# A top-2-of-8 expert layer: tokens as the stationary operand, weights streamed 512 columns wide as rounded high and low halves

## The reference

```
probs = softmax(h @ w_router);  top_p, top_i = top_k(probs, 2);  top_p /= sum(top_p)
gates = sum(one_hot(top_i, 8) * top_p)
out = sum over the 8 experts e of gates[e] * ((silu(h @ wg[e]) * (h @ wu[e])) @ wd[e])
```

## Time and profile before

| | us |
|---|---|
| median of three runs (2529.94 to 2535.5) | 2533.66 |
| the profiled execution: its time | 2536.45 |
| its span in the trace | 2534.8 |
| TensorE busy (87% of the span) | 2208.2 |
| VectorE busy (28%) | 713.9 |
| ScalarE busy (20%) | 515.2 |
| first expert matmul starts at | 1815.36 |
| last store of expert rows is issued at | 2486.20 |
| mean granted TensorE clock over the span | 0.901 |

### The profile page before, as it was taken

One profiled execution on the slowest core, in us unless ns is written; L12 is line 12 of the kernel. 1 busy time (PEld: TensorE's weight loads), 2 busy tenths in 40 slices (PEclk: granted clock), 3 DMA queues, 4 the chain that ended last, 5 costly groups with the idle time before them and its releaser, 6 DMA issues.

```text
span 2534.8 us, 35841 instructions
## 1 busy us (share of the span) xinstructions
PE 2208.2 (87%) x14774; PEld 1990.0 (79%) x14774; DVE 713.9 (28%) x1347; ACT 515.2 (20%) x1094; POOL 242.6 (10%) x325
## 2 busy tenths in 40 slices
PE   5899898976769999997898699997699999999992
PEld 4788787864659999996654576686699999999991
DVE  2245555537232222222234344402100000000003
ACT  1133422203022212211123233301211111111101
POOL 0000101020002302300020023200100000000001
PEclk8899999956789999998898689977799999999996
DMA  7222100030213242332070256510788988898883
GB/s 192 69 67 75 35 1 4 1 95 26 83 33 92 72 113 76 88 103 71 15 245 1 67 193 237 179 50 1 202 216 211 267 211 211 208 271 215 209 203 123
DMA packets 452952, 306.17 MB, mean 121 GB/s; under 512 B 22381, under 2 KB 435456, under 8 KB 448704
## 3 DMA queue, kind: packets, MB, share of 16 engines
q1 hardware_dynamic: 433812, 225.76, 34.2%
q0 software_dynamic: 19024, 78.72, 9.4%
HBM read 276.44 MB, written 28.14 MB: 120 GB/s over the span
## 4 chain that ended last, share of the span: by engine, by line
PE 66%; issue 19%; DVE 6%; POOL 4%; DMA 2%; SPq 1%; ACT 1%; POOLq 0%; DVEq 0%; ACTq 0%
PE bank L1197 17%; PE bank L526 13%; PE bank L1226 8%; PE bank L1038 3%; POOL actL L2220 2%; PE bank L706 2%; PE bank L691 1%; PE bank L701 1%; PE bank L1052 1%; PE bank L1079 1%; PE bank L564 1%; POOL actH L2217 1%; SPq L2311 1%; PE bank L857 1%; PE bank L859 1%
## 5 line engine op out<-in xcount | busy, mean ns | idle before, releaser
L1197 PE MATMUL bank<-arena,w_ring 128*128 128x176 f32 x2816 | 424.4, 314 | 4.8 <-issue 4.8
L1197 PEld LDWEIGHTS bank<-arena,w_ring 128*128 128x128 f32 x2816 | 422.3, 191 | 6.8 <-issue 6.8
L526 PE MATMUL bank<-hT,w_ring 128*128 128x260 f32 x1600 | 362.8, 389 | 16.2 <-DVE hT L1249 15.1
L526 PEld LDWEIGHTS bank<-hT,w_ring 128*128 128x128 f32 x1600 | 309.3, 194 | 66.0 <-DVE hT L1249 16.0
L1790 ACT ACTIVATE arena<-bank 128x512 f32<-128x512 f32 (+5 forms) x284 | 135.7, 494 | 511.5 <-PE bank L526 225.6
L1226 PE MATMUL bank<-arena 128*128 128x176 f32 x1408 | 220.1, 313 | 0.0
L1226 PEld LDWEIGHTS bank<-arena 128*128 128x128 f32 x1408 | 210.2, 190 | 0.2
L857 PE MATMUL bank<-hH,gu_high 128*128 128x260 f32 x704 | 143.6, 286 | 18.3 <-DVE w_low L1508 18.3
L1752 DVE TENSOR_TENSOR arena<-arena,bank 128x176 f32<-128x176 f32 x88 | 29.8, 338 | 431.6 <-PE bank L1197 431.6
L859 PE MATMUL bank<-hL,gu_high 128*128 128x260 f32 x704 | 143.0, 285 | 0.0
L861 PE MATMUL bank<-hH,w_low 128*128 128x260 f32 x704 | 142.9, 285 | 0.0
(11 more groups left out here) (440 smaller groups left out, 2884.6 us busy)
## 6 DMA issues: line engine op xcount, KB each, us to landing
w_ring<-in_we_gate SPq DMA_DIRECT2D x88, 512.0 KB, 7.2
w_ring<-in_we_up SPq DMA_DIRECT2D x88, 512.0 KB, 7.3
arena<-in_we_down SPq DMA_DIRECT2D x64, 704.0 KB, 6.6
w_ring<-in_w_in_a SPq DMA_DIRECT2D x26, 512.0 KB, 3.8
w_ring<-in_w_gate SPq DMA_DIRECT2D x22, 512.0 KB, 3.9
w_ring<-in_w_up SPq DMA_DIRECT2D x22, 512.0 KB, 3.9
arena<-in_w_down SPq DMA_DIRECT2D x16, 704.0 KB, 6.2
slots<-arena POOLq DMA_DIRECT2D x4, 2560.0 KB
```

The lines of the kernel that those rows point to most:

```text
L526: mm = pe.matmul(out[i][:, 0:hi - lo], w_ring[:, s, kt, :], rhs[:, kt, lo:hi], start=(kt == 0), stop=(kt == KT - 1))
L1197: mm = pe.matmul(bank[bk][:, 0:SLOTS], w_ring[:, s, kt, :], hTe[:, kt, :], start=(kt == 0), stop=(kt == KT - 1))
```

## The change

SLOTS becomes 192, so a pass is 128 tokens and a tail (TAIL) of 64. The roles in the matmul are exchanged: the tokens are the stationary operand, and the weights stream past, 512 columns (in the last piece 384) at a time.

- The weights of a pass come in 35 chunks instead of 30 blocks: 24 for gate and up (three pieces of the 1408 columns, 512, 512 and 384; a chunk has two row blocks of 128 for one piece) and 11 for down (128 rows of all 1024 columns). A row of a chunk is 512, 384 or 1024 floats in one run of memory; before, a run was 128 floats. The ring has RAWS = 18 slots of 1024 floats: the 11 of `w_ring`, and seven more in `hT` and `xT`, which are free by then.
- ScalarE rounds every chunk into one of HIGHS = 6 buffers (`high_part`), VectorE writes the remainder over the raw chunk (`low_part`). Both run EAHEAD = 4 chunks ahead of TensorE in the program's order; the four chunks that open the next pass are done at the end of the present one, those of the first pass ahead of the loop.
- The tokens, and later the activations, are transposed into tiles of twice SLOTS columns: 192 high, then 64 low of the tail, then 128 low of the first 128 tokens.
- A product of one 128-row block with one 512-column stretch is five matmuls (`products`): high tokens x high weights, low tokens x high weights, the tail's high and low together (128 stationary columns) x high weights, high tokens x low weights, the tail's high x low weights. The low half of the tail comes out on partitions 64 to 127 of its bank and is added later.
- At the end of each of the three pieces (chunks 7, 15 and 23), ScalarE and VectorE form silu(gate) x up for the 128 tokens and for the tail. TensorE transposes the result three or four chunks later (TURN_AFTER: after chunks 11, 19 and 26), and the next pass's tokens after chunks 28 and 30.
- Results come out as rows of tokens: the transposes of the results, and the copies around them, are gone. A pass's rows are written in two DMAs.
- SyncE no longer waits for the scatters ahead of the first weights, only for the table and for the last use of the slots by the output projection; the four first chunks go out ahead of the loop, the next fourteen as soon as the transposes of the stream are over.

```
-SLOTS = 176
+SLOTS = 192
 ROWS = SLOTS // 2
+TAIL = SLOTS - P
+PIECES = [(0, 512), (512, 1024), (1024, FE)]
+GU_CHUNKS = 8 * len(PIECES)
+CHUNKS = GU_CHUNKS + FB
+TURN_AFTER = {11: (0, 2), 19: (2, 4), 26: (4, 6), 28: (6, 8), 30: (8, 10)}
...
+ACT0 = DENSE_PARTS * 2 * FB + 1
+LAPS = CHUNKS + 1
+RAWS = LAPS // 2
+HIGHS = 6
+EAHEAD = 4
...
+        def raw_slot(m):
+            s = m % RAWS
+            if s < WS:
+                return w_ring[:, s].rearrange("p k c -> p (k c)")
+            rest, i = (hT, s - WS) if s < WS + 4 else (xT, s - WS - 4)
+            return rest.rearrange("p k t -> p (k t)")[:, i * D:(i + 1) * D]
...
-                        for kt in range(KT):
-                            mm = pe.matmul(bank[bk][:, 0:SLOTS], w_ring[:, s, kt, :], hTe[:, kt, :],
-                                           start=(kt == 0), stop=(kt == KT - 1))
...
+                    def products(out, tail, x, at, top, low, first, last):
+                        w = x[:, at]
+                        pe.matmul(out, w[:, 0:P], top, start=first, stop=False)
+                        pe.matmul(out, w[:, SLOTS + TAIL:WIDE], top, start=False, stop=False)
+                        pe.matmul(tail, w[:, P:SLOTS + TAIL], top, start=first, stop=False, skip_group_check=True)
+                        pe.matmul(out, w[:, 0:P], low, start=False, stop=last)
+                        return pe.matmul(tail[0:TAIL], w[:, P:SLOTS], low, start=False, stop=last, skip_group_check=True)
...
+                    for i, (lo, hi) in enumerate(PIECES):
+                        n = hi - lo
+                        at = 4 * (i % 2)
+                        if i == 1:
+                            pe.wait_ge(y_read, p * 4 + 4)
+                        if i == 2:
+                            pe.wait_ge(h_split, p * TURNS + KT + 4 + 2)
+                        for q in range(4):
+                            for k in range(2):
+                                kt = 2 * q + k
+                                c = slice(k * n, (k + 1) * n)
+                                for j in range(2):
+                                    m = 8 * i + 2 * q + j
+                                    if k == 0:
+                                        pe.wait_ge(split, p * LAPS + SPLIT0 + m + 1)
+                                    mm = products(bank[at + j][:, 0:n], bank[at + 2 + j][:, 0:n], hTw, kt, e_high[:, m % HIGHS, c],
+                                                  low_slot(m)[:, c], kt == 0, kt == KT - 1)
+                                    if k == 1:
+                                        mm.then_inc(e_used, 1)
+                            turns(m)
+                    pe.wait_ge(h_split, p * TURNS + KT + 4 + 4)
+                    for f in range(FB):
+                        m = GU_CHUNKS + f
+                        pe.wait_ge(split, p * LAPS + SPLIT0 + m + 1)
+                        pe.wait_ge(h_split, p * TURNS + KT + 4 + f // 2 + 1)
+                        for j in range(2):
+                            c = slice(512 * j, 512 * (j + 1))
+                            mm = products(bank[4 + j], bank[6 + j], actTw, f, e_high[:, m % HIGHS, c], low_slot(m)[:, c],
+                                          f == 0, f == FB - 1)
+                        mm.then_inc(e_used, 1 if f < FB - 1 else 2)
+                        turns(m)
...
+            def low_part(m, lap):
+                n = chunk_columns(m)
+                dve.wait_ge(high, lap + SPLIT0 + m + 1)
+                dve.tensor_tensor(low_slot(m)[:, 0:n], raw_slot(m)[:, 0:n], e_high[:, m % HIGHS, 0:n].bitcast(F32), ALU.subtract)\
+                   .then_inc(split, 1 if m < CHUNKS - 1 else 2)
...
+                dve.tensor_tensor(to[:, :, SLOTS:SLOTS + TAIL], v[:, :, P:SLOTS], to[:, :, P:SLOTS].bitcast(F32), ALU.subtract)
+                dve.tensor_tensor(to[:, :, SLOTS + TAIL:WIDE], v[:, :, 0:P], to[:, :, 0:P].bitcast(F32), ALU.subtract).then_inc(h_split, 1)
...
+                            dve.wait_ge(silu_done, p * 7 + 2 * i + 1)
+                            dve.tensor_tensor(actu[0:TAIL, 0:n], actu[0:TAIL, 0:n], tu[0:TAIL], ALU.add)
+                            dve.tensor_tensor(actg[0:TAIL, 0:n], actg[0:TAIL, 0:n], tg[0:TAIL], ALU.add).then_inc(act_split, 1)
+                            dve.tensor_tensor(acte[:, 0:n], acte[:, 0:n], bu, ALU.mult)
+                            dve.wait_ge(silu_done, p * 7 + 2 * i + 2)
+                            dve.tensor_tensor(actg[0:TAIL, 0:n], actg[0:TAIL, 0:n], actu[0:TAIL, 0:n], ALU.mult).then_inc(act_split, 1)
...
+                act.wait_ge(e_used, lap + RAWS + m - HIGHS + 1)
+                act.activation(e_high[:, m % HIGHS, 0:n], raw_slot(m)[:, 0:n], ACT.Copy)\
+                   .then_inc(high, 1 if m < CHUNKS - 1 else 2)
...
+                    for m in range(LAPS):
+                        if m + EAHEAD < CHUNKS:
+                            high_part(m + EAHEAD, p * LAPS, p)
+                        elif m + EAHEAD >= LAPS:
+                            high_part(m + EAHEAD - LAPS, p * LAPS + LAPS, p + 1)
...
+                            act.wait_ge(e_used, p * LAPS + RAWS + m + 1)
+                            act.activation(actg[0:TAIL, 0:n], tg[TAIL:P], ACT.Copy)
+                            act.activation(actu[0:TAIL, 0:n], tu[TAIL:P], ACT.Copy)
+                            act.activation(acte[:, 0:n], bg, ACT.Silu).then_inc(silu_done, 1)
+                            act.wait_ge(act_split, p * 6 + ACT0 + 2 * i + 1)
+                            act.activation(actg[0:TAIL, 0:n], actg[0:TAIL, 0:n], ACT.Silu).then_inc(silu_done, 1)
...
-            sp.wait_ge(spread, 160)
+            def expert_chunk(m, e):
+                dst = raw_slot(m)[:, 0:chunk_columns(m)]
+                if m < GU_CHUNKS:
+                    lo, hi = PIECES[m // 8]
+                    q = m % 8 // 2
+                    w = a["we_up" if m % 2 else "we_gate"][0][bass.ds(e, 1), 2 * q * P:2 * (q + 1) * P, lo:hi]
+                    load(dst.rearrange("p (k c) -> p k c", k=2), w.rearrange("a (k p) c -> p (a k) c", p=P), e_loaded[m % RAWS])
+                else:
+                    f = m - GU_CHUNKS
+                    w = a["we_down"][0][bass.ds(e, 1), f * P:(f + 1) * P, :]
+                    load(dst, w.rearrange("a p c -> p (a c)"), e_loaded[m % RAWS])
...
+            filled(sp, (("o", 1, KT - 1), 1))
+            for m in range(EAHEAD):
+                expert_chunk(m, e0)
...
+                    for m in range(EAHEAD, CHUNKS):
+                        if m != GU_CHUNKS:
+                            sp.wait_ge(e_used, p * LAPS + (m + 1 if m != GU_CHUNKS - 1 else m + 2))
+                        expert_chunk(m, e)
+                    after = sp.value_load(table[0:1, bass.ds(p + 1, 1)], min_val=0, max_val=NE - 1)
+                    for m in range(EAHEAD):
+                        sp.wait_ge(e_used, p * LAPS + LAPS + m + 1)
+                        expert_chunk(m, after)
```

More of the change, by code:

```diff
@@ L1168, in _, with turn_tokens @@
                     mm.then_inc(full("upto"), 1)
-            def expert_tokens(g, b):
+            for b in range(8):
+                pe.wait_ge(bank_free[b], uses[b])
+            pe.wait_ge(table_ready, 1)
+            n_passes = pe.value_load(table[0:1, PASSES + 1:PASSES + 2], min_val=1, max_val=PASSES)
+            def turn_tokens(g, at):
+                pe.wait_ge(h_split, at + KT - 1)
+                b = bank[TURN_BANK[6 + g]]
                 for j in range(2):
@@ L1174, in expert_tokens, with turn_act @@
                                           hrow[0:ROWS, r, (2 * g + j) * P:(2 * g + j + 1) * P], ident[0:ROWS, 0:ROWS])
-                mm.then_inc(hx, 1)
+                mm.then_inc(turned_out, 1)
+            def turn_act(g, at):
+                pe.wait_ge(h_split, at + KT - 1)
+                b = bank[TURN_BANK[g]]
+                lo = PIECES[g // 2][0]
+                for j in range(min(2, FB - 2 * g)):
+                    c = slice((2 * g + j) * P - lo, (2 * g + j + 1) * P - lo)
+                    pe.transpose(b[:, j * SLOTS:j * SLOTS + P], acte[:, c], ident)
+                    mm = pe.transpose(b[:, j * SLOTS + P:(j + 1) * SLOTS], actg[0:TAIL, c], ident[0:TAIL, 0:TAIL])
+                mm.then_inc(turned_out, 1)
@@ L1177, in _ @@
             pe.wait_ge(hrow_in, 16)
             for g in range(4):
[L1179 to L1187, removed]
+                turn_tokens(g, g)
@@ L1231, in _, with turns @@
-                    results(KT - 1)
+                    def turns(m):
+                        if m not in TURN_AFTER:
+                            return
+                        first, last = TURN_AFTER[m]
+                        if first < 6:
+                            pe.wait_ge(act_split, p * 6 + ACT0 + first + 2)
+                        elif first == 6:
+                            pe.wait_ge(hrow_in, p * 16 + 32)
+                        for g in range(first, last):
+                            if g < 6:
```

(11 more changed lines are left out.)

205 lines of the change are left out of this document (105 added, 100 removed).

## The result

The changed kernel takes 2542.55 us (median of 8 runs, 2540.92 to 2546.24) against 2533.36 us before: a ratio of 1.004, 95% interval 1.0029 to 1.0051. It is 9.2 us slower; 2489 was predicted, in a range of 2472 to 2520.

A forecast was written before the change was run, and what follows sets the result against it. The expert stage was taken as bound by the columns TensorE streams. A pass of 71.2 + 3.8 + 1.5 = 76.5 us saves 8 x 6.96 = 55.7, less 10 + 1: 2489 us, range 2472 to 2520.

The forecast's parts named there:

- The matmuls: Expert pass: 270 matmuls of 512 columns at 215.7 ns and 80 of 384 at 162.4, 71.2 us a pass.
- The 149 ns stream: Old expert matmul instructions, 176 columns at two clocks each: 146.7 ns plus 2.4, taken as the new matmuls' surplus.
- Transposes: Expert pass: 38 transposes replace 32, 11 at 0.11 us and 27 at under 0.1, at most 3.8 us.
- The rest of the pass: Loop's head, end of the pass and short waits: 1.5 us a pass, kept as before.
- Splitting beside TensorE: ScalarE's 50 us and VectorE's 58 us a pass hide behind TensorE, in time by 0.6 us at the first piece's end.
- Rival 2: Piece ends of the expert pass don't hold and TensorE stalls: 2582 us, mild form 2505; chance 0.10 in its slower form.
- Weights fit: Expert pass: the same 17.3 MB in 76 us, 245 GB/s with the token rows, loaded fourteen chunks or 30 us ahead.
- Rival 3: DMA engines give no more than before in a pass, so it still takes 83 us: 2545 us; chance 0.06.
- Rival 1: Expert matmuls each carry a fixed 11.3 ns surplus, so a pass takes 79.6 us: 2514 us; chance 0.15.
- Rival 4: Successive matmuls overlap, 512 columns cost far less than 512 clocks, and VectorE sets the pass: 2381 us; chance 0.02.
- Ahead of the loop: Early weight loads share the DMA engines with scatters and row fetch: 10 us more, between 3.2 and 14.6.
- The end: End of the last pass: two copies, a tail addition and a second store issue replace less work, 1 us more.

The follow-up runs named there:

- run 2: The changed kernel with four weight chunks still loaded early and the other 14 waiting until the first pass's rows have landed: 2537.82 us, ratio to before 1.0020.

## Why the prediction was wrong, step by step

**The step that failed** is the choice in "The matmuls": "Since the surplus is absent at half clock, it isn't a rate per column. It is either fixed per matmul, or the weight load of 128 columns, which is hidden once the moving side is longer." The conclusion doesn't follow, and both branches were wrong. A rate that lies between the two clocks is absent at the lower one and present at the upper. The starts now known at full clock, 119.6 ns for 260 columns, 175.6 for 384 and 232.8 for 512, lie on a line of 0.449 ns per column and 2.8 ns beside it. Over the 2.4 ns and one column per clock, the surplus is 8.9, 13.2 and 17.1 ns: 0.033 to 0.034 ns per column at each length, so neither fixed nor bound to the weights. At half clock the first products of the changed kernel show no surplus:

```profile
1820.23 0.63 PE L1268 MATMUL bank<-e_high,hTw 128*128 128x512 f32 x1
...
1822.37 0.63 PE L1268 MATMUL bank<-e_high,hTw 128*128 128x512 f32 x1
```

Five matmuls in 2.14 us, 428 ns each; 512 clocks at 1.2 GHz are 426.7. The granted clock there is 0.50. With 2 bytes the surplus is gone at full clock too. The 149 ns stream that decided the choice couldn't tell either: its 176 columns take 0.85 ns each, so a limit of 0.449 ns would not show in them. The 17.1 and 13.2 ns are 5.7 us a pass, 45 in all, of the 53.5 by which the forecast missed. That the surplus grows with the columns, and that it goes away with 2-byte operands, is shown. The edit changed the type of the weights' halves and of the tokens' together, so which side sets the limit, and whether bytes or the number format do, stays open.

**Transposes**: "at most 3.8 us" a pass. It was 6.5, because they alternate between two sizes, while the rows I took the price from the earlier trace rows show one size at a time. 2.7 us a pass, 22 in all; it was the second term mis-sized. **The rest of the pass**, kept at 1.5 us, is about 0.0, which gives 12 back: by luck that hides 12 of the 67 us that the other two cost. Per pass 5.7 + 2.7 - 1.5 = 6.9 us, and 83.39 - 76.5 is 6.9.

**Splitting beside TensorE**: right. Between the first store and its last matmul TensorE has no wait at all in the trace, at the pieces' ends neither; VectorE is busy for 54 us a pass (58 worked out) and ScalarE for 48 (50). Rival 2 is refuted. **Weights fit**: right; 227 GB/s in a pass, and 252 when a pass takes 75 us. Rival 3, whose 2545 is nearest to the result, is refuted as a mechanism: the time came out near it by other terms. Rival 1 had the direction, but its fixed 11.3 ns is contradicted by 384 and 512 columns. Rival 4: no stream went below a column per clock, with 2 bytes and 512 columns neither (215 ns). That is also against the 131 ns that the Trainium skill ("TensorE: Matmul & The Clock Gate", section "Back-to-back issue gap") states for such a stream of weight loads and matmuls.

**Ahead of the loop**: 10 us predicted between 3.2 and 14.6, 9.1 measured, and mostly in the scatters, as argued; the 10 itself was a choice between two bounds. One reading under it was off: the fetch's 7.7 us before already had weights beside it, issued 1.7 us after it. With none beside it, in run 2, the fetch took 5.84. **The end**: 1 us predicted; the two stretches around the first and last store sum to 0.6.

## What to carry to other kernels

Take the price of a matmul from a stream of the same operand type at two lengths before scaling it to a third: a surplus that vanishes at half clock may well grow with every column. Keep transposes of one size together, and with 2-byte operands keep stationary tiles 128 columns wide: each change of size cost about 0.1 us here, and TensorE's matmuls show no wait for it. With 4-byte operands the change of width cost nothing. When a wait is taken away, ask who needs the work that then starts early, and let only that much start.

## What the runs showed of the hardware that was not expected

- At full clock TensorE takes rounded 4-byte columns (fp32r) at 0.449 ns each, as worked out above from 260, 384 and 512 of them; 2-byte columns (bf16) take 215 ns for 512 and 162.3 for 384. At half clock 512 columns of fp32r take 428 ns, one column per clock.
- With 2-byte operands a change between 128 and 64 stationary columns costs 94 ns ahead of the 64-column matmul and 119 ns behind it; with 4-byte operands the starts stay 232 to 233 ns apart whether the fifth matmul has 64 or 128.
- Transposes that alternate between 128 and 64 rows take 0.224 us each, in runs of one size 0.115 (0.92 us for eight).
- 2 MB of weights issued beside the 4.3 MB of scatters delayed the row fetch by 4.8 us, 9.2 MB by 6.5 to 7.3.
